# Six PSUM banks and three staging tiles, instead of eight and four, for the gate/up stage of four feed-forward blocks

## The reference

```
mod = silu(c) @ w_mod[l] + b_mod[l]              # shifts, scales and gates for the layer
h = rmsnorm(x) * (1 + sc) + sh                   # (256, 1024)
x = x + 0.5 * g * ((silu(h @ w_gate) * (h @ w_up)) @ w_down)    # width 1024 -> 2816 -> 1024
```

## Time and profile before

| | us |
|---|---|
| median of three runs | 1575.04 |
| the profiled execution | 1575.6 |
| its span, first to last instruction | 1573.8 |
| TensorE busy with matmuls | 1484.4 (94%) |
| VectorE busy | 1012.6 (64%) |
| ScalarE busy | 696.3 (44%) |
| GpSimd busy | 300.6 (19%) |
| mean granted TensorE clock | 0.971 |

### The profile page before, as it was taken

One profiled execution on the slowest core, in us unless ns is written; L12 is line 12 of the kernel. 1 busy time (PEld: TensorE's weight loads), 2 busy tenths in 40 slices (PEclk: granted clock), 3 DMA queues, 4 the chain that ended last, 5 costly groups with the idle time before them and its releaser, 6 DMA issues.

```text
span 1573.8 us, 18935 instructions
## 1 busy us (share of the span) xinstructions
PE 1484.4 (94%) x7424; PEld 1132.6 (72%) x7424; DVE 1012.6 (64%) x1519; ACT 696.3 (44%) x1112; POOL 300.6 (19%) x269
## 2 busy tenths in 40 slices
PE   6998899998889999999889999899999999989999
PEld 1746546754678888786478888788887865778887
DVE  0377595853558888355477887678885553777654
ACT  3414432043346563352255564456643531465552
POOL 0050328001401110043231110011100240311100
PEclk9999898997899999999999999999999999999999
DMA  9534254232257989432347988479895423378551
GB/s 341 181 107 160 81 172 164 81 134 95 106 187 268 318 291 378 145 111 81 108 136 264 320 308 325 136 257 318 302 356 176 134 81 107 115 243 271 170 204 54
DMA packets 164297, 306.41 MB, mean 195 GB/s; under 512 B 7280, under 2 KB 117488, under 8 KB 154352
## 3 DMA queue, kind: packets, MB, share of 16 engines
q1 hardware_dynamic: 161072, 299.48, 55.3%
q10 hardware_dynamic: 3136, 5.72, 1.0%
HBM read 304.11 MB, written 1.08 MB: 194 GB/s over the span
## 4 chain that ended last, share of the span: by engine, by line
PE 79%; DVE 10%; ACT 5%; POOL 2%; DMA 2%; issue 1%; ACTq 0%; DVEq 0%; POOLq 0%
PE ps L438 78%; PE ps L441 2%; DMA ring<-in_w_mod_dram 1%; DVE H L1842 1%; DVE arena L1208 1%; DVE arena L1205 1%; ACT arena L1472 1%; DVE H L1791 0%; DVE misc L1505 0%; DMA ctab<-in_consts_dram 0%; DVE arena L2657 0%; DVE arena L1194 0%; POOL arena L2396 0%; DVE H L1776 0%; DVE X L1782 0%
## 5 line engine op out<-in xcount | busy, mean ns | idle before, releaser
L438 PE MATMUL ps<-hh,whi 128*128 128x512 f32 x1408 | 488.0, 400 | 5.7 <-DVE hh L2024 5.7
L2018 DVE TENSOR_TENSOR wlo<-ring,whi 128x1024 fp32r<-128x1024 f32 x264 | 322.0, 1231 | 153.2 <-ACT whi L1957 151.5
L1957 ACT ACTIVATE whi<-ring 128x1024 fp32r<-128x1024 f32 x264 | 274.3, 1055 | 229.7 <-PE ps L438 211.6
L438 PE MATMUL ps<-hh,wlo 128*128 128x256 f32 x1408 | 367.7, 282 | 0.0
L438 PEld LDWEIGHTS ps<-hh,whi 128*128 128x128 f32 x1408 | 254.4, 190 | 55.5 <-DVE hh L2024 6.7
L438 PEld LDWEIGHTS ps<-hh,wlo 128*128 128x128 f32 x1408 | 268.3, 191 | 16.9
L438 PE MATMUL ps<-ring,H 128*128 128x512 f32 (+1 forms) x544 | 236.6, 586 | 10.5 <-ACT arena L2159 5.6
L438 PEld LDWEIGHTS ps<-ring,H 128*128 128x128 f32 x544 | 102.4, 195 | 118.0 <-issue 103.2
L548 DVE SCALAR_TENSOR_TENSOR ring<-ring,cb 128x1024 f32<-128x1024 f32 x144 | 178.1, 1238 | 4.4 <-DMA ring<-in_mods_dram 4.0
L438 PE MATMUL ps<-H,ring 128*128 128x256 f32 (+1 forms) x576 | 157.8, 433 | 1.6 <-DVE H L1842 0.7
L2007 POOL TENSOR_TENSOR alo<-H,ahi 128x256 fp32r<-128x256 f32 x88 | 70.5, 801 | 462.0 <-ACT ahi L1995 458.5
(11 more groups left out here) (339 smaller groups left out, 1568.3 us busy)
## 6 DMA issues: line engine op xcount, KB each, us to landing
ring<-in_mods_dram SPq DMA_DIRECT2D x76, 1024.0 KB, 5.7
ring<-in_w_in_dram SPq DMA_DIRECT2D x48, 1024.0 KB, 5.1
ring<-in_ffn_w_gate_dram SPq DMA_DIRECT2D x44, 1024.0 KB, 5.5
ring<-in_ffn_w_up_dram SPq DMA_DIRECT2D x44, 1024.0 KB, 7.2
ring<-in_ffn_w_down_dram SPq DMA_DIRECT2D x44, 1024.0 KB, 6.4
ring<-in_w_out_dram SPq DMA_DIRECT2D x12, 1024.0 KB, 5.0
ring<-in_w_mod_dram SPq DMA_DIRECT2D x8, 1024.0 KB, 17.8
gates<-gate_rows SPq DMA_DIRECT2D x7, 512.0 KB, 6.0
```

Source lines behind the costliest of these rows:

```text
L438: return self.e.matmul(o, lhsT, rhs, start=start, stop=stop)
L1957: a.done(a.e.activation(hi, M.slot(key)[:, r0:r0 + rn, :], ACT.Copy), ("whi", l, sub, n))
L2018: v.done(v.e.tensor_tensor(lo, M.slot(key)[:, r0:r0 + rn, :], plain(hi), ALU.subtract), ("split", l, sub, n), *([M.freed(key)] if ends els ...
```

## The change

The pool "ga" has six banks, 0 to 5, so a block takes the banks of the block three before it (four before, when there were eight). Its turn counter is no longer set back: a feed-forward asks for 44 banks, and 44 mod 6 is 2, so the feed-forwards begin at turns 0, 2, 4 and 0. The pool "down" is banks 2 to 5 (it was 4 to 7), and "turnf" is 6, 7, 0, 1 (it was 0 to 3). SG has three tiles, and ScalarE's copy of block x waits for the ALO of block x - 3 (x - 4 before).

```diff
-... "ga": range(8),
-         "down": (4, 5, 6, 7), ... "turnf": (0, 1, 2, 3), ...
+... "ga": range(6),
+         "down": (2, 3, 4, 5), ... "turnf": (6, 7, 0, 1), ...
 def spare(M):
-    return [M.H[:, 2 * i:2 * i + 2, 256:512] for i in range(4)]
+    return [M.H[:, 2 * i:2 * i + 2, 256:512] for i in range(3)]
...
-            a.wait_ge(key, ("alo", l, sub, x - 4))
-            a.done(a.e.activation(SG[x % 4], M.psum[:, b:b + 2, 256:512], ACT.Copy), ("copied", l, sub, x))
+            a.wait_ge(key, ("alo", l, sub, x - 3))
+            a.done(a.e.activation(SG[x % 3], M.psum[:, b:b + 2, 256:512], ACT.Copy), ("copied", l, sub, x))
...
 def pe_ffn(pe, l, sub):
     M = pe.M
-    pe.turn["ga"] = 0
     for f in range(0, 22, 2):
```

More of the change, by code:

```diff
@@ L202 @@
 NS = 5
-POOLS = {"all": range(8), "six": range(6), "mods": (6, 7), "rest": (0, 1), "att": (2, 3, 4, 5), "bo": (7,), "sq": (4, 5, 6, 7), "low": (0, 1), "skk": (2,), "sdec": (4, 5), "sq2": (6, 7), "ga": range(8),
-         "down": (4, 5, 6, 7), "chain": (2, 3, 4, 5), "proj": (0, 1), "rec": (2, 3), "sd": (4, 5, 6), "dbo": (7,), "outx": (2, 3, 0, 1), "ds": (4, 5, 6, 7), "turnf": (0, 1, 2, 3), "turnx": (6, 7, 4, 5)}
+POOLS = {"all": range(8), "six": range(6), "mods": (6, 7), "rest": (0, 1), "att": (2, 3, 4, 5), "bo": (7,), "sq": (4, 5, 6, 7), "low": (0, 1), "skk": (2,), "sdec": (4, 5), "sq2": (6, 7), "ga": range(6),
+         "down": (2, 3, 4, 5), "chain": (2, 3, 4, 5), "proj": (0, 1), "rec": (2, 3), "sd": (4, 5, 6), "dbo": (7,), "outx": (2, 3, 0, 1), "ds": (4, 5, 6, 7), "turnf": (6, 7, 0, 1), "turnx": (6, 7, 4, 5)}
 class Store:
@@ L1986, in act_ffn @@
             b = M.banks[key, 0]
-            a.wait_ge(key, ("alo", l, sub, x - 4))
-            a.done(a.e.activation(SG[x % 4], M.psum[:, b:b + 2, 256:512], ACT.Copy), ("copied", l, sub, x))
+            a.wait_ge(key, ("alo", l, sub, x - 3))
+            a.done(a.e.activation(SG[x % 3], M.psum[:, b:b + 2, 256:512], ACT.Copy), ("copied", l, sub, x))
         for x in pair:
             a.wait_ge(("summed", l, sub, x))
-            a.done(a.e.activation(SG[x % 4][:, 0, :], SG[x % 4][:, 0, :], ACT.Silu), ("silu", l, sub, x))
+            a.done(a.e.activation(SG[x % 3][:, 0, :], SG[x % 3][:, 0, :], ACT.Silu), ("silu", l, sub, x))
         for j, x in enumerate(pair):
-            i = x % 4
+            i = x % 3
             a.wait_ge(("act", l, sub, f + j))
@@ L2006, in pool_ffn @@
         g.wait_ge(("ahi", l, sub, f))
-        g.op(g.e.tensor_tensor(M.ALO[:, f, :], SG[f % 4][:, 0, :], plain(M.AHI[:, f, :]), ALU.subtract), ("alo", l, sub, f))
+        g.op(g.e.tensor_tensor(M.ALO[:, f, :], SG[f % 3][:, 0, :], plain(M.AHI[:, f, :]), ALU.subtract), ("alo", l, sub, f))
 def v_ffn(v, l, sub, work):
@@ L2035, in v_ffn @@
         for j in range(2 if isinstance(f, int) else 0):
-            i, key = (f + j) % 4, ("gu", l, sub, f + j)
+            i, key = (f + j) % 3, ("gu", l, sub, f + j)
             b = M.banks[key, 0]
@@ L2041, in v_ffn @@
         for j in range(2 if isinstance(f, int) else 0):
-            i = (f + j) % 4
+            i = (f + j) % 3
             v.wait_ge(("silu", l, sub, f + j))
```

## The result

The changed kernel takes 1583.45 us (median of six runs, 1581.67 to 1588.46) against 1574.67 us before (median of six, 1570.93 to 1576.45). Fifteen runs of the changed kernel against those of before give the ratio 1.0067, with a 95% interval of 1.0050 to 1.0086, so 7.9 to 13.5 us slower. The profiled execution took 1586.83 us, its span is 1585.0 us, 11.2 us longer than before. The forecast was 1587 us with a range of 1580 to 1594, and 11.8 us on 1575.6 is a ratio of 1.0075.

The account below looks back on a forecast made before the run. The prediction took TensorE, busy 1484 of 1573.8 us, as the bound. Pair waits of 5.1 us plus down-start waits of 6.7 us made 11.8 us on 1575.6: forecast 1587 us, range 1580 to 1594.

Parts of the forecast that it names:

- TensorE's waits in the feed-forwards land on the end one for one: In FF1 to FF4 TensorE waits for nobody, so any matmul held back there lengthens the whole time by as much.
- The pairs' waits: An odd block's first matmul waits for the previous pair's even-block add: 16 pairs at 0.26 us, two in FF2 together 0.9.
- the rule: A waiting matmul costs how late its add ends after the matmul's earlier start, plus 0.16 us (0.06 + 0.10).
- The term for FF2: Pairs' waits in FF2: blocks 0, 4, 8, 16 at 0.26 us each, block 12 at 0.72, block 10 at 0.18.
- that for FF4: Pairs' waits in FF4: the pairs beginning at blocks 0 and 4, 0.26 us each.
- The down starts: The first down matmul waits for the add of block 20 or 21: 1.7, 2.3, 2.3, 0.5 us in FF1 to FF4, sum 6.7.
- Tiles cost nothing: ScalarE's copy waiting for the ALO of three blocks before costs nothing, with 5.5 us to spare.
- The sum, 11.8 us: Whole loss: 5.1 us of waits in the pairs plus 6.7 us at the starts of the down stages.
- rival 2: Clock falls after idles of about 2 us at FF1 to FF3 down starts (1592), or pair waits cost 0.50 (1591); chance 0.16.
- Rival 3: Clock falls through the gate/up stages, a slow stretch at each of 18 pair waits, 31 us more: 1618 us; chance 0.03.
- Rivals 1 and 4: Rival 1: only the down stage waits, 1582 us, chance 0.12. Rival 4: all waits vanish, 1575.6 us, chance 0.05.
- Rival 5: Not slower: half-clock time over the program shrinks by more than 24 us; at 24 us the time is 1575.6; chance 0.04.

Follow-up runs that it names:

- e8_kept_busy: Kernel before with unread products where TensorE idles between the parts (11 before each part's second transposed block, 5 before the first gate/up matmul): 1566.31 us, ratio 0.9960.
- e9_changed_busy: Changed kernel with unread products (11 and 5 per part) where TensorE idles between the parts: 1579.5 us, ratio 1.0037 to the kernel before.
- e1_down_moved: Changed kernel with the down stage on banks 6, 7, 2, 3, turnf on 4, 5, 0, 1 and the turn set back per feed-forward: 1578.0 us, ratio 1.0025.
- e7_turn_reset: Changed kernel with the turn of the six banks set back to 0 at each feed-forward: 1584.59 us, ratio 1.0074 to the kernel before.
- e10_busy_down: Changed kernel with unread products between the parts and 5, 7, 7 and 0 more in the waits at the down starts: 1578.39 us, ratio 1.0036.
- e3_two_tiles: Kernel before with two staging tiles in place of four, banks as before: 1571.84 us, ratio 0.9991.
- e2_eight_down_waits: Kernel before, eight banks and four tiles, but the down stage on banks 2 to 5 and turnf on 6, 7, 0, 1: 1583.16 us, ratio 1.0056.
- e4_product_later: Changed kernel with the modulation product of a pair's third quarter put off until after the adds: 1580.46 us, ratio 1.0037 to the kernel before.
- e6_four_banks: Kernel before with four banks for gate and up in place of eight, four tiles, down stage on banks 4 to 7: 1615.26 us, ratio 1.0269.

## Why the prediction was right

- *TensorE's waits in the feed-forwards land on the end one for one.* Shown: nothing later in the feed-forwards makes up for them. After its wait the down stage of FF1 takes 60.15 us where it took 60.05, and in every kernel here the time of a feed-forward is 184.1 us (that of `e8_kept_busy`) plus its waits and slow stretches.
- *The pairs' waits: 18 of them, 5.1 us.* The mechanism and nearly all sizes were right: 17 waits, 4.7 us by the gate/up stages of `e9_changed_busy` against `e8_kept_busy`. 16 cost 0.26 us, block 12 of FF2 among them, where the trace of before had given 0.72; block 10 of FF2 had no wait where 0.18 was foreseen. Why VectorE was late at these two in the profile of before stands below this list. Block 4 of FF4 waits 0.54 us in each of the four other profiles of that order (`e1_down_moved`, `e7_turn_reset`, `e9_changed_busy`, `e10_busy_down`) as in the changed kernel, 0.28 more than by the rule: the high part ahead of that pair's last split comes later there. It comes 0.28 us later at block 12 of FF3 in `e3_two_tiles` too, which has no such waits. Why stays open. The term for FF2 was too large by 0.6 us and that for FF4 too small by 0.28; that they offset each other in part is luck.
- *The down starts: 1.7, 2.3, 2.3 and 0.5 us.* Measured by the gap between the last gate/up matmul and the first of the down stage, with the 0.10 us to the next: 1.65, 2.25, 2.3 and 0.5.
- *Tiles cost nothing.* Shown with two of them.
- *The sum, 11.8 us.* The waits alone measure 11.3 us once the slow stretches at the starts are out of the way. That the profiled execution lost nearly the same, 11.2 us, is luck, since its sum is another: 11.4 us of waits, plus 3.2 us for two slow stretches at the down starts, less 0.9 us at the starts of the feed-forwards and 2.5 us in the rest of the program. The clock behind the down starts, which the sum left to rival 2, cost 0 to 3.2 us in the profiles.
- *Rival 2* (the clock follows the down start's waits) was half right: it did after the two idles of 2.0 us of the profiled execution, not after those of 1.40 and 0.3, and over all profiles with such an idle it did in some and not in others. Its other half, 0.50 us for a wait in the pairs, fell to 0.26. *Rival 3* is refuted for this kernel: in the changed kernel no slow stretch stands in a gate/up stage away from its start, and even 40 waits of up to 1.7 us left the clock at 1.00 there. The Trainium skill (page "TensorE: Matmul & The Clock Gate", section "A second HAM failure mode: psum-queue depth-cycling") tells of a kernel that cycled through PSUM banks and whose clock oscillated for its short idles; the trace does not agree for these waits. *Rivals 1 and 4* fall with `e1_down_moved`. *Rival 5* named something that does happen: slow stretches elsewhere cost the profiled execution of the changed kernel some 3.4 us less than that of before. It is too small to make good 11 us. The spread of the runs is not explained by the starts alone: the five runs of `e8_kept_busy` lie within 2.7 us and the 17 of before beside them within 7.5, but the nine runs of `e9_changed_busy`, with the same products, lie within 7.4.

The two late adds of FF2 (blocks 10 and 12) go back to weights that landed late. In the kernel before, ScalarE stood idle in the pair that begins at block 10 until the gate weights and the up weights had come (timeline of before, ScalarE):

```profile
888.05 2.01 ACT L1957 ACTIVATE whi<-ring 128x1024 fp32r<-128x1024 f32 x2 [1.94 <-DMA ring<-in_ffn_w_gate_dram]
...
891.05 1.06 ACT L1957 ACTIVATE whi<-ring 128x1024 fp32r<-128x1024 f32 x1 [0.98 <-DMA ring<-in_ffn_w_up_dram]
```

The splits and the adds behind these idles came later, by 0.7 us at block 10, and VectorE made up only part of it by block 12. The add of block 12 ends 0.57 us after the matmul's start there, 0.53 in `e2_eight_down_waits` and 0.41 in `e3_two_tiles`, which have eight banks too, and 0.10, the common value, in `e8_kept_busy`. So it was not the chance of one execution. In the changed kernel ScalarE has nearly the same idles (1.65 and 0.97 us), and yet block 10 brings no wait and block 12 the common 0.26; how VectorE makes it good there was not followed.

## What to carry to other kernels

When a pool of buffers gets shallower, ask for each user how long before it the buffer's last reader ended, and go through all repeats: an add that is 0.1 us late in two pairs of five costs more than its lateness, since 0.16 us come with each wait, from the end of the add to the matmul and from that matmul to the next. A ring whose length no longer divides the number of requests makes later stages start on other, younger buffers, so a stage that takes several buffers at once is to be given those that were free longest. And where the matmul engine idles for about 2 us between stages, a few unread products there can save a slow stretch of 1.6 us. Between the parts they made the kernel 4.1 to 8.5 us faster; at the down starts no gain could be told by the times.

## What was not expected of the hardware

- An idle of 2.0 us at a down start was followed by 3.4 us at the lower clock twice in the changed kernel and twice in `e9_changed_busy`, and never in the three of `e2_eight_down_waits`, with the same matmuls behind it. The idle of 1.79 us in `e4_product_later` had one behind it too. What decides is open. Seven idles of 1.4 to 1.5 us at down starts and seventeen of 1.5 us in `e6_four_banks` had none. Such a stretch costs 1.6 us here.
- The slow stretches at the starts of the feed-forwards, which the change did not touch, cost 4.8 us in the profile of before (185.64 + 185.78 + 185.69 + 184.10 against 4 x 184.1), nearly half of what the change costs. In the profile of `e3_two_tiles`, where nothing differs at these starts, they cost 1.9 us.
